# MLP hidden slices by feature with held weights, bias rows in two parts, and attention heads begun inside projections, in a fused twelve-stage kernel

## What is computed

```
def sq_relu_mlp(h, w1, b1, w2, b2):          # D_FF = 4096, twice
    a = jax.nn.relu(h @ w1 + b1)
    return (a * a) @ w2 + b2

# attention, twice: 8 heads of 128 (the first with a rotary part of 64)
s = where(causal, q @ k.T * scale, -1e30)
p = softmax(s)
o = p @ v

# recurrent block: (h * gelu(yb)) @ w_out + b_out
```

## Time and profile before

| | |
|---|---|
| median of 3 runs | 1750.84 us |
| time of the profiled execution | 1750.2 us |
| its span (first to last instruction) | 1748.6 us |
| PE busy | 1646.2 us, 94% |
| VectorE busy | 1147.3 us, 66% |
| ScalarE busy | 839.1 us, 48% |
| chain that ended last, share of PE | 71% |
| mean granted TensorE clock | 0.969 of 2.4 GHz |

### The profile page before, as it was taken

One profiled execution on the slowest core, in us unless ns is written; L12 is line 12 of the kernel. 1 busy time (PEld: TensorE's weight loads), 2 busy tenths in 40 slices (PEclk: granted clock), 3 DMA queues, 4 the chain that ended last, 5 costly groups with the idle time before them and its releaser, 6 DMA issues.

```text
span 1748.6 us, 20517 instructions
## 1 busy us (share of the span) xinstructions
PE 1646.2 (94%) x8221; PEld 1327.7 (76%) x8221; DVE 1147.3 (66%) x1354; ACT 839.1 (48%) x1134; POOL 153.8 (9%) x293
## 2 busy tenths in 40 slices
PE   7778999988988999999999999999999999799998
PEld 3656787875677788878888868888788888578887
DVE  4699778888969665575546876544754546665554
ACT  3553465544234555544335875334634435553433
POOL 4510100026600100000000000000000000000000
PEclk9878999999999999999999989999999999899999
DMA  9838588752036566445654554555555554245551
GB/s 305 310 126 308 185 302 332 288 214 100 1 142 220 193 227 238 161 168 192 225 184 141 199 189 171 192 192 169 207 178 183 186 188 167 96 144 193 193 191 74
DMA packets 145096, 335.45 MB, mean 192 GB/s; under 512 B 18213, under 2 KB 34061, under 8 KB 143850
## 3 DMA queue, kind: packets, MB, share of 16 engines
q1 hardware_dynamic: 134310, 293.65, 48.8%
q0 software_dynamic: 9696, 37.29, 5.6%
q10 hardware_dynamic: 996, 3.20, 0.5%
HBM read 328.86 MB, written 6.83 MB: 192 GB/s over the span
## 4 chain that ended last, share of the span: by engine, by line
PE 71%; DVE 16%; ACT 5%; issue 4%; POOL 2%; DMA 1%; SPq 1%; DVEq 0%; ACTq 0%; POOLq 0%
PE ps L670 22%; PE ps L672 22%; PE ps L671 22%; DVE wlo L1794 3%; PE ps L755 2%; ACT whi L1253 1%; DMA operands<-in_mod_mix_w 1%; PE ps L749 1%; DVE work L2247 1%; DVE xlo L1799 1%; PE ps L762 1%; DVE B L1927 1%; POOL mod L2509 1%; DVE B L1926 1%; DVE small L1859 1%
## 5 line engine op out<-in xcount | busy, mean ns | idle before, releaser
L1794 DVE TENSOR_TENSOR wlo<-raw,whi 128x2048 fp32r<-128x2048 f32 (+2 forms) x247 | 559.8, 2283 | 253.5 <-ACT whi L1253 252.2
L1253 ACT ACTIVATE whi<-raw 128x2048 fp32r<-128x2048 f32 (+2 forms) x247 | 466.9, 1908 | 233.9 <-PE ps L672 170.5
L670 PE MATMUL ps<-whi,xhi 128*128 128x512 f32 (+2 forms) x1244 | 477.5, 384 | 18.9 <-DVE xlo L1799 17.3
L672 PE MATMUL ps<-whi,xlo 128*128 128x512 f32 (+2 forms) x1244 | 471.8, 379 | 0.0
L671 PE MATMUL ps<-wlo,xhi 128*128 128x512 f32 (+2 forms) x1244 | 471.7, 379 | 0.0
L670 PE MATMUL ps<-whi,hhi 128*128 128x512 f32 x736 | 294.6, 400 | 6.2 <-DVE hlo L1799 5.2
L671 PE MATMUL ps<-wlo,hhi 128*128 128x512 f32 x736 | 289.0, 393 | 0.0
L672 PE MATMUL ps<-whi,hlo 128*128 128x512 f32 x736 | 288.8, 392 | 0.0
L670 PEld LDWEIGHTS ps<-whi,xhi 128*128 128x128 f32 x1244 | 235.5, 189 | 64.6 <-DVE xlo L1799 21.0
L672 PEld LDWEIGHTS ps<-whi,xlo 128*128 128x128 f32 x1244 | 235.5, 189 | 44.2
L671 PEld LDWEIGHTS ps<-wlo,xhi 128*128 128x128 f32 x1244 | 235.8, 190 | 41.7
(11 more groups left out here) (371 smaller groups left out, 1599.8 us busy)
## 6 DMA issues: line engine op xcount, KB each, us to landing
raw<-in_mlp_w SPq DMA_DIRECT2D x64, 1024.0 KB, 5.6
raw<-in_ffn_w_gate SPq DMA_DIRECT2D x44, 1024.0 KB, 5.1
raw<-in_ffn_w_up SPq DMA_DIRECT2D x44, 1024.0 KB, 5.2
raw<-in_ffn_w_down SPq DMA_DIRECT2D x44, 1024.0 KB, 4.9
mod<-in_mod_ffn_w POOLq DMA_DIRECT2D x16, 1024.0 KB, 6.9
mod<-in_mod_mix_w POOLq DMA_DIRECT2D x12, 1024.0 KB, 7.4
operands<-in_mod_mix_w SPq DMA_DIRECT2D x8, 1024.0 KB, 8.5
raw<-in_lru_w_in SPq DMA_DIRECT2D x8, 1024.0 KB, 5.2
```

Of the source, the lines that this page charges most:

```text
L670: pe.matmul(o, lh, rh, start=start, stop=False)
L672: return pe.matmul(o, ll, rh, start=False, stop=stop)
L1253: act.activation(whi[:, c % SPL, 0:n], raw[:, c % RAW, 0:n], ACT.Copy).then_inc(hi_done, 1)
L1794: dve.tensor_tensor(wlo[:, c % RAW, 0:n], raw[:, c % RAW, 0:n], whi[:, c % SPL, 0:n].bitcast(F32), ALU.subtract).then_inc(lo_done, 1)
```

## The change

1. **MLP slices 2 to 7 by feature.** Both chunks of `w1` of such a slice are loaded as 8x256 columns and multiplied by `columns`; the result has features as rows, so its `token_copy` and `token_turn` are gone (`TURNED` of the MLPs falls from 8 to 2). ScalarE applies bias and relu in 2 instructions of 256 columns per feature half (`hidden_features`), and VectorE's `hlo` goes by feature half. The product of slice i+1 stands whole ahead of `down` of slice i.
2. **Bias rows in parts, in the MLPs.** The bias row is split by ScalarE (`brow_hi`, 1x1024) and VectorE (`brow_lo`, 1x1024), both put between chunks 4 and 5 of the stage, and added by 8 matmuls of 512 columns inside the first `down`, behind its waits. `open_acc` is left to "lru", where it moves ahead of `turned(3)`.
3. **Softmax scaling on ScalarE.** In both attentions VectorE takes the reciprocal alone, and ScalarE multiplies (two instructions) behind the exponentials of the next head.
4. **Heads begun earlier.** In "mla" the rotary turn of the first four heads stands inside the second query projection, that of the others behind the scores of head 0, and the waits for them go with them. In "att" the scores of heads 0, 1 and 2 stand inside and behind the last query projection; ScalarE's chunk copies move ahead of the last `token_copy`, and VectorE's low part of chunk 6 moves into iteration 0.

```
-TURNED = {n: (2 if n == "kv" else k) for n, k in SLICES.items()}
+TURNED = {n: (2 if n in ("kv", "mlp0", "mlp1") else k) for n, k in SLICES.items()}
...
-                    chunks[mlp_up(name, i, h)] = (up_src(t["mlp_w1"][l], i, h), HALF)
+                    chunks[mlp_up(name, i, h)] = (up_src(t["mlp_w1"][l], i, h), HALF) if i < 2 else (ws_src(t["mlp_w1"][l], 2 * i + h), COLS)
...
+                        if biased and k == 0:
+                            half = slice(512 * n, 512 * (n + 1))
+                            pe.matmul(ps[:, 2 * tt + n, :], ones_r[0:1, :], brow_hi[:, half], start=True, stop=False)
+                            last = pe.matmul(ps[:, 2 * tt + n, :], ones_r[0:1, :], brow_lo[biased][:, half], start=False, stop=False)
...
                     if i:
+                        columns(mlp_up(name, i + 1, 0), slice_bank(i + 1, 0))
+                    if i < 2:
                         for tt in range(T):
-                            project(name, mlp_up(name, i + 1, 0), slice_bank(i + 1, tt), tt, 0)
+                            token_turn(name, i, tt)
+                    if i:
+                        columns(mlp_up(name, i + 1, 1), slice_bank(i + 1, 1))
+                    else:
+                        for tt in range(T):
+                            project(name, mlp_up(name, 1, 1), slice_bank(1, tt), tt, 1)
                     for tt in range(T):
-                        token_turn(name, i, tt)
-                    for tt in range(T):
-                        project(name, mlp_up(name, i + 1, 1), slice_bank(i + 1, tt), tt, 1)
-                    if i == 0:
-                        open_acc(name)
-                    for tt in range(T):
-                        pe.wait_ge(hid_ok, HID0[name] + 2 * i + tt + 1)
-                        down(mlp_down(name, i, 0), 4 * (i % 2), tt)
-                        if i == 6 and tt == 0:
-                            for t2 in range(T):
-                                token_turn(name, 7, t2)
+                        if i == 0:
+                            acc_ready(name, tt)
+                            pe.wait_ge(brow_lo_ok, MLPS.index(name) + 1)
+                        pe.wait_ge(hid_ok, HID0[name] + 2 * i + (tt if i < 2 else 0) + 1)
+                        down(mlp_down(name, i, 0), 4 * (i % 2), tt, biased=name if i == 0 else None)
+                    pe.wait_ge(hid_ok, HID0[name] + 2 * i + 2)
...
+                    if g:
+                        turn_rotary(0)
...
-                pe.wait_ge(q_ok, 4)
-                pe.wait_ge(qt_ok, 2)
+                pe.wait_ge(q_ok, 2)
+                pe.wait_ge(qt_ok, 1)
                 attention(0, qT, kT, V, True)
...
+                if i == 0:
+                    turn_rotary(1)
                 if i == 1:
+                    pe.wait_ge(q_ok, 4)
+                    pe.wait_ge(qt_ok, 2)
                     same_step()
...
-                turned(3)
                 pe.wait_ge(lg_ok, KT)
                 open_acc("lru")
+                turned(3)
                 pe.wait_ge(hg_lo, 1)
...
-                for tt in range(T):
-                    project("att", c + 3, slice_bank(1, tt), tt, 1)
+                project("att", c + 3, slice_bank(1, 0), 0, 1)
+                acc_ready("att", 1)
+                pe.wait_ge(feat_ok, FEAT0["att"] + 2)
+                scores(1, 0, qT2, kT2, False)
+                scores(1, 1, qT2, kT2, False)
+                project("att", c + 3, slice_bank(1, 1), 1, 1)
+                scores(1, 2, qT2, kT2, False)
...
+                if l == 0:
+                    act.activation(ones_r[:, :], ones[0:1, :], ACT.Copy)
+                act.wait_ge(brow_in, 16 * (l + 1))
+                act.activation(brow_hi[:, :], brow[name], ACT.Copy).then_inc(brow_hi_ok, 1)
                 hi(c + 5)
...
+                    if 1 <= i <= HEADS:
+                        s = (i - 1) % 3
+                        act.wait_ge(rc_ok, HEADS * n + i)
+                        for tt, (lo, up) in enumerate(((0, P), (P, 3 * P))):
+                            last = act.activation(sms[:, s, lo:up], sms[:, s, lo:up], ACT.Copy, scale=recips[:, 2 * s + tt:2 * s + tt + 1])
+                        last.then_inc(p_ok, 1)
...
                 for j in range(3, 6):
                     lo(c + j)
+                    if j == 4:
+                        dve.wait_ge(brow_hi_ok, MLPS.index(name) + 1)
+                        rest(brow_lo[name][:, :], brow[name], brow_hi[:, :]).then_inc(brow_lo_ok, 1)
...
-                        do(dve.reciprocal(newton[:, 0:2], atts[:, 2 * s:2 * s + 2]))
-                        dve.tensor_scalar(sms[:, s, 0:P], sms[:, s, 0:P], newton[:, 0:1], None, ALU.mult)
-                        dve.tensor_scalar(sms[:, s, P:3 * P], sms[:, s, P:3 * P], newton[:, 1:2], None, ALU.mult).then_inc(p_ok, 1)
-                        dve.wait_ge(p_ok, e + 1)
+                        dve.reciprocal(recips[:, 2 * s:2 * s + 2], atts[:, 2 * s:2 * s + 2]).then_inc(rc_ok, 1)
```

More of the change, by code:

```diff
@@ L138, in order_of_halves @@
             each(c + 9, c + 11)
+        elif name in ("mlp0", "mlp1"):
+            for k in range(3, n - 3):
+                both(c + k, c + k + 1) if k >= 6 and k % 4 > 1 else each(c + k, c + k + 1)
         else:
@@ L708, in project_narrow, with down @@
                 last.then_inc(pe_pass, 1)
-            def down(c, tile, tt, first=False, final=False, src=(hhi, hlo)):
+            def down(c, tile, tt, first=False, final=False, src=(hhi, hlo), biased=None):
                 chunk_ready(c)
@@ L965, in mla, with turn_rotary @@
                 spread_third(1, (6, 7))
+            def turn_rotary(g):
+                pe.wait_ge(qp_ok, g + 1)
+                for r in range(2):
+                    for tt in range(T):
+                        last = pe.transpose(ps[:, 4 * g + 3, r * L + tt * P:r * L + (tt + 1) * P], qp_tok[:, g, tt, r * P:(r + 1) * P], ident[:, :])
+                last.then_inc(qt_ps, 1)
             def z_pass(c, tt):
@@ L1506, in mla @@
                     act.activation(qpT[:, 2 * g:2 * g + 2, :].rearrange("p r l -> p (r l)"), ps[:, 4 * g + 3, :], ACT.Copy).then_inc(qt_ok, 1)
-                hi(5)
+                    if g == 0:
+                        hi(5)
                 attention(0)
@@ L1716, in att @@
                 hi(c + 4)
-                hi(c + 5)
                 for tt in range(T):
                     feature_copy("att", 0, tt, qT2)
-                for tt in range(T):
-                    token_copy("att", 1, tt, c + 3, x_scale("ffn11", tt))
+                hi(c + 5)
+                token_copy("att", 1, 0, c + 3, x_scale("ffn11", 0))
                 hi(c + 6)
+                token_copy("att", 1, 1, c + 3, x_scale("ffn11", 1))
                 for tt in range(T):
@@ L2187, in attention @@
                         piece(6)
+                    if n and i == 0:
+                        lo(FIRST["att"] + 6)
             def s5():
@@ L2361, in att @@
                 c = FIRST["att"]
-                for j in range(3, 7):
+                for j in range(3, 6):
                     lo(c + j)
```

77 lines of the change are left out of this document (52 added, 25 removed).

## The result

The changed kernel takes **1765.63 us** (median of 6 runs, 1759.46 to 1768.91) against 1750.57 us before (6 runs, 1749.12 to 1753.19), a ratio of 1.0083 with the interval [1.0064, 1.0101]. It is some 15 us slower. Forecast were 1753.5 us and a range to 1759. The sign of the change was right, its size was not, and the time lies outside the range.

The account below looks back on a forecast made before the run. PE was taken as the bound, 94% busy, each PE instruction in the MLPs costing its pitch. Terms 7.7 - 10.7 - 1.1 + 5.9 + 0.8 + 0.6 - 0.5 + 0 = +2.7 on 1750.84 gave 1753.5 us, range 1746.5 to 1759.

Parts of the forecast that it names:

- the pitch of 0.120 per matmul: MLP slices 2 to 7: 256-column matmuls 0.120 us apart, making feature chunks 0.32 us dearer each, +7.7 us over 24.
- the wait of 1.07 us that went: "mlp0", slice 2: PE's wait for VectorE's low part disappears, -1.1 us.
- the total of -4.1: MLP slices by feature: +7.7 for chunks, -10.7 for turns removed, -1.1 for the wait in slice 2.
- the row's low part pushes that start: MLP heads: the bias row's low part joins VectorE's list and delays the first `down` by 1.15 us per MLP.
- I take 0.4 each: MLP heads: extra loss from PE restarting at half clock after the longer wait, +0.8 us for both.
- 8 bias matmuls of 0.227: First `down` of each MLP: eight short bias matmuls now stand behind the wait and cost 1.8 us.
- rival (1): MLP heads and "lru" tail: half-clock restarts cost more, 1.6 us per head and +2 in "lru"; 1757.3 us, chance 0.22.
- Forecast 0 in "att": "att": longer head loop +2.6, earlier start -2, shorter VectorE lists -0.6; net 0 us, between -3 and +2.5.
- The loop's +0.6 per head: "att", head 4 onward: scaling on ScalarE lengthens the loop by 0.65 us per head, +2.6 over four heads.
- VectorE's shorter lists would repay 0.6: "att", heads 0 to 3: VectorE's shorter instruction lists gain 0.6 us.
- In "mla" the step: "mla": fewer VectorE multiplications and earlier scores, limited by ScalarE's wait for POOL; -0.5 us, between -3.5 and +2.5.
- +0.6 forecast: "lru": earlier accumulator matmuls gain at most 1.5 us, set against a half-clock restart of 2.1; between -1.5 and +2.

Follow-up runs that it names:

- columns_only: The kernel before with only the change of MLP slices 2 to 7 to feature form: 1746.74 us, ratio 0.9975.
- together_behind: The changed kernel with its 8 bias matmuls still behind the hidden-slice wait, but one after the other ahead of all 48 products: 1758.11 us, ratio 1.0047.
- strewn_128_rows: The changed kernel with the 8 bias matmuls replaced in place by 8 on 128 rows, leaving out the second bias: 1756.70 us, ratio 1.0032.
- parts_ahead: The changed kernel with the 8 bias matmuls together ahead of the wait for the hidden slice: 1750.90 us, ratio 1.0003.
- filler_12: The changed kernel with 12 plain one-row matmuls of 256 columns put into PE's 5.78 us of idle time: 1766.09 us, ratio 1.0086.
- hidden_first: The changed kernel with VectorE's residual of the stage before moved behind slice 0's square and `hlo`, both MLPs: 1744.27 us, ratio 0.9961.
- bias_back: The changed kernel with `open_acc` for the MLPs again ahead of the hidden-slice wait and no split bias row: 1749.43 us, ratio 0.9985.
- scaling_in_mla_only: The changed kernel with unsplit bias rows, `open_acc` ahead again, and the softmax scaling of "att" back on VectorE: 1744.84 us, ratio 0.9966.
- columns_and_heads: The kernel before with feature slices 2 to 7 and the earlier heads in both attentions, scaling left on VectorE: 1743.62 us, ratio 0.9964.
- columns_and_lru: The kernel before with feature slices 2 to 7 and the new place of `open_acc` in "lru": 1746.31 us, ratio 0.9979.
- filler_rows_128: The changed kernel with 12 plain 128-row matmuls of 256 columns put into PE's idle time before the first `down`: 1753.91 us, ratio 1.0018.
- the two combined kernels: The changed kernel with residual moved later, "lru" and "att" scaling restored; bias matmuls strewn behind the wait (1737.65 us) or all ahead (1735.59 us).
- combined_ahead: The changed kernel with residual moved later, "lru" and "att" scaling restored, all 8 bias matmuls ahead of the wait: 1735.59 us, ratio 0.9919.

## Why the prediction was wrong

**What held.** In the slices the pitch of 0.120 per matmul, the 0.27 us less per slice and the wait of 1.07 us that went; the total of -4.1, against -4.2 in columns_only, is partly luck. The other slices of "mlp0" show -5.3 where 6 x 0.27 + 1.07 = 2.7 were due: before, the last 84 products took 21.5 us with 19.0 due at their pitch, at a granted clock of 1.00, because of the waits for VectorE shown under columns_only. The forecast did not have these 2.5 us, nor the 2.0 that "s5" lost. What also held is the reading that VectorE sets the start of the first `down`, that `open_acc` ran in time that was free, and that the row's low part pushes that start: +1.4 and +1.5 against 1.15, with PE idle for 5.78 us where 5.7 were forecast. POOL is slowed beside VectorE's pieces: its two pairs take 3.47 and 4.34 us in place of 2.60 and 3.48, and ScalarE's copy starts 2.3 us later. The Trainium skill's rule, "SBUF — State Buffer", section "SBUF: two separate sides", says so, and this trace agrees: VectorE's L1993 and L1994 take 1.72 to 2.19 us beside these pairs and 1.27 to 1.28 behind them. The "att" heads are 3.98 us apart, 4.0 forecast. The wait in "lru" for `hlo` is 5.11 us and ends at 1028.5 once the shift is taken off, forecast 1028.4; the 1.54 us ahead of it were not forecast.

**The step that failed** is the clock behind the wait, "I take 0.4 each", together with the price of the bias matmuls, "8 bias matmuls of 0.227". For both MLPs:

| term of the first `down`, two MLPs | forecast | from the traces |
|---|---|---|
| later start | +2.3 | +2.9 |
| 8 bias matmuls at 0.227 | +3.6 | +3.6 |
| changes between one row and 128: 14.29 - 12.70, twice | 0 | +3.2 |
| clock: 21.31 - 14.29 and 18.07 - 14.29, less 2.88 and 1.49 before | +0.8 | +6.4 |
| sum | +6.7 | +16.1 |

These 9.4 us more than forecast are most of the 12.7 by which the profiled run (+15.4) missed the +2.7. I had rival (1), the restart at half clock, at 1757.3 and at 0.22, with its upper bound set at the 8 bias matmuls at half clock, 1.6 us each. The bound was made on the assumption that the slow stretch ends by itself after a time like those of the earlier trace rows, and that one-row matmuls in it merely run slower. together_behind, strewn_128_rows and parts_ahead show that it does end 5 to 5.6 us after the first product *if the products stand together or all have 128 rows*. Strewn one-row matmuls hold it off: the loss by clock is 7.0 and 3.8 us in the changed kernel, 2.7 in each MLP of parts_ahead, where PE also had no work on 128 rows for 5.7 us. So of 10.8 us some 5.4 come with the stretch ahead and 5.4 with the strewing.

The 15 and the 9 slow matmuls of the earlier trace rows, from which I argued for and against rival (1), do not belong to "mlp0" and "mlp1". In all seven profiles with `open_acc` ahead of the wait one first `down` loses 1.5 to 1.8 us by the clock and the other 2.7 to 3.0. Before it was "mlp0" that lost more; in the other six it is "mlp1". The two belong together, 4.3 to 4.8 us in sum.

The fillers also suggest why the 5.8 us of idle time were not the main thing. Before, PE did one-row matmuls for 3.72 us and waited 0.8. In view of filler_12 this was for the clock nearly the same as standing still, so that the time without products on 128 rows grew only from 4.5 us (194.65 to 199.17) to 5.8, not from 0.8 to 5.8. All seven kernels with `open_acc` ahead start the first `down` at half clock behind a wait of 0.4 to 0.8 us; hidden_first, with a wait of 0.62 and nothing of one row ahead of it, starts at full clock. No run takes `open_acc` away and changes nothing else. In the earlier trace rows it was to be seen that the clock was low after a wait of only 0.8; I noted it and did not ask what the 3.72 us ahead had been.

**The attentions and "lru".** Forecast 0 in "att", +2.0 in the profile: the scaling costs 3.3 us by the profiles of bias_back and scaling_in_mla_only, and the heads begun earlier give back 1.9 by those of columns_and_heads and columns_only. The loop's +0.6 per head was right; that VectorE's shorter lists would repay 0.6 was not seen. The 0.34 and 0.40 of the earlier trace rows are means that take in one head of "mla" where both instructions took 1.15; in "att" they take 0.29 and 0.35. In "mla" the step stays open. The stretch from its first 512-column product behind 60 us to its first `down` took 70.3 us before and in columns_only, 72.0 in columns_and_lru. In the eleven kernels with the whole change of "mla" it took 68.6 once (filler_rows_128), 69.4 to 69.6 five times (the changed kernel among them) and 72.4 to 72.5 five times. Nothing in that stage differs between them, so one profile each can't tell a gain or a loss of 0.5 there, and 3 us between two kernels' medians can come from it. "lru" (+1.6 in the profile, +0.6 forecast) does not show in the medians.

**"ffn10"**, where nothing was changed, shows +1.5 us. The profiles point to chance in the clock. From 766.76 to the head of "lru" at 955.97 the kernel before takes 189.2 us, and so do ten others, parts_ahead, together_behind and the two combined kernels, with the same "ffn10", among them; the changed kernel takes 190.7, filler_12, filler_rows_128, hidden_first and strewn_128_rows 190.6 to 192.1. In the changed kernel eight products behind the turn start 0.43 us apart.

## What to carry to other kernels

Before giving a short matmul a new place, ask what it does to the stream around it. One-row matmuls cost twice here, by every change between one row and 128 and by holding the clock down after a wait. So put them together and ahead of a wait, not among the products. When PE stands for another engine, look what that engine does first that nobody is waiting for: moving four residual instructions took 21 us off the changed kernel.

## What the runs showed of the hardware

- Twelve plain matmuls of one row in place of an idle time of 5.8 us left the clock at 0.50 (1766.1 us); the same twelve on 128 rows kept it at the first product (1753.9 us).
- After an idle time of 5.8 us, or 3.5 us behind eight one-row matmuls, the clock came back 5 to 5.6 us after the first product, when all matmuls had 128 rows (parts_ahead, strewn_128_rows). With a pair of one-row matmuls ahead of every bank it stayed low for 15.8 us in "mlp0" and 8.6 us in "mlp1".
- The clock also fell while PE was busy, 2.5 to 2.7 us into a first `down` with strewn one-row matmuls, and was back 3.4 us later ("mlp1" of hidden_first, "mlp0" of filler_rows_128).
- A pair of one-row matmuls among products of 128 rows costs 0.4 us more than its own pitch at full clock (14.29 us for 56 matmuls, 12.70 at their pitch); one after another they follow each other at 0.23 (combined_ahead).
